# Expert weights in larger adjacent pieces: 4 KB of gate and up, 8 KB of down, a strided read of the columns, and sorted row counts in both layers

## The reference

```python
def grouped_moe(h, router_w, router_bias, w_gate, w_up, w_down, sh_gate, sh_up, sh_down):
    ...                                   # sigmoid scores, best group of four experts, top 2 in it
    out = swiglu(t, sh_gate, sh_up, sh_down)            # the shared expert, every token
    for e in range(N_EXPERTS):                          # 16
        out = out + combine[:, e:e + 1] * swiglu(t, w_gate[e], w_up[e], w_down[e])
def swiglu(t, wg, wu, wd):
    return (jax.nn.silu(t @ wg) * (t @ wu)) @ wd        # wg, wu: 1024 x 512, wd: 512 x 1024
```

## Time and profile before

| | |
|---|---|
| median of three runs | 1674.37 us |
| the profiled execution's own time | 1667.71 us |
| its span, first to last instruction | 1665.8 us |
| TensorE busy | 1504.8 us, 90% |
| VectorE, ScalarE, GpSimd busy | 528.6, 393.8, 187.7 us |
| mean granted TensorE clock | 0.961 of full speed |
| moved by DMA | 334.6 MB, mean 201 GB/s |
| sparse steps of layer 0 | from 784.7 us, about 284 us |
| sparse steps of layer 1 | from 1340.8 to 1631.8 us |

### The profile page before, as it was taken

One profiled execution on the slowest core, in us unless ns is written; L12 is line 12 of the kernel. 1 busy time (PEld: TensorE's weight loads), 2 busy tenths in 40 slices (PEclk: granted clock), 3 DMA queues, 4 the chain that ended last, 5 costly groups with the idle time before them and its releaser, 6 DMA issues.

```text
span 1665.8 us, 31618 instructions
## 1 busy us (share of the span) xinstructions
PE 1504.8 (90%) x13895; PEld 868.5 (52%) x13895; DVE 528.6 (32%) x934; ACT 393.8 (24%) x930; POOL 187.7 (11%) x207
## 2 busy tenths in 40 slices
PE   4799888999988999799999999978989899999996
PEld 2434444454545444455555555545647865555555
DVE  3254555445433121224112112141352412111213
ACT  2211333333434200210122122112241212122111
POOL 0000034133332200000000100000000010100100
PEclk9599999999989999889999999998999899999998
DMA  7355334333330622015999999961302189999972
GB/s 275 127 185 191 126 104 149 104 125 127 127 127 26 170 82 76 3 51 214 388 373 362 377 370 380 361 215 56 109 1 77 66 321 391 372 361 358 366 258 85
DMA packets 161871, 334.62 MB, mean 201 GB/s; under 512 B 14083, under 2 KB 61883, under 8 KB 155579
## 3 DMA queue, kind: packets, MB, share of 16 engines
q1 hardware_dynamic: 148795, 308.77, 52.3%
q0 software_dynamic: 7104, 12.60, 2.2%
q10 hardware_dynamic: 5824, 11.11, 1.9%
HBM read 327.58 MB, written 16.65 MB: 207 GB/s over the span
## 4 chain that ended last, share of the span: by engine, by line
PE 84%; ACT 6%; DVE 5%; DMA 3%; issue 1%; SPq 0%; DVEq 0%; ACTq 0%; POOLq 0%
PE ps L1365 19%; PE ps L1076 10%; PE ps L1395 10%; PE ps L1093 7%; PE ps L1288 7%; PE ps L1319 5%; PE ps L1027 3%; PE ps L1181 2%; PE ps L1600 2%; PE ps L1409 2%; PE ps L1512 2%; PE ps L1046 2%; PE ps L1129 1%; ACT aT L736 1%; PE ps L1168 1%
## 5 line engine op out<-in xcount | busy, mean ns | idle before, releaser
L1365 PE MATMUL ps<-ring,ssb 128*32 128x256 f32 x3472 | 193.3, 379 | 1.6 <-ACT ssb L891 1.6
L1076 PE MATMUL ps<-aT,ring 128*128 128x512 f32 x384 | 175.4, 606 | 0.0
L1365 PEld LDWEIGHTS ps<-ring,ssb 128*32 128x32 f32 x3472 | 113.9, 110 | 75.0 <-ACT ssb L891 1.8
L2010 DVE COPY big<-ps 32x256 f32<-32x256 f32 x190 | 80.5, 424 | 201.6 <-PE ps L1395 199.5
L1076 PEld LDWEIGHTS ps<-aT,ring 128*128 128x128 f32 x384 | 71.6, 194 | 84.3 <-issue 84.2
L1395 PE MATMUL ps<-ring,ssb 128*32 128x256 f32 x1808 | 105.4, 389 | 11.0 <-ACT ssb L903 11.0
L1093 PE MATMUL ps<-aT,ring 128*128 128x512 f32 x256 | 114.2, 595 | 0.0
L908 ACT COPY big<-ps 32x256 f32<-32x256 f32 x190 | 68.8, 362 | 179.7 <-PE ps L1395 177.9
L1288 PE MATMUL ps<-big,ring 128*128 128x512 f32 x256 | 110.2, 592 | 0.0
L2003 DVE TENSOR_TENSOR ssb<-ssb,ps 128x384 f32<-128x384 f32 (+2 forms) x32 | 17.6, 551 | 267.1 <-ACT ssb L899 267.1
L808 ACT ACTIVATE ssb<-ps,ncum 128x128 f32<-128x128 f32 x256 | 73.3, 371 | 98.5 <-PE ps L1156 97.6
(11 more groups left out here) (293 smaller groups left out, 1875.8 us busy)
## 6 DMA issues: line engine op xcount, KB each, us to landing
ring<-in_ada_w SPq DMA_DIRECT2D x48, 1024.0 KB
ring<-in_moe_w_gate SPq DMA_DIRECT2D x75, 512.0 KB, 9.2
ring<-in_moe_w_up SPq DMA_DIRECT2D x75, 512.0 KB, 12.1
ring<-in_moe_w_down SPq DMA_DIRECT2D x37, 1024.0 KB, 10.3
ring<-in_ssd_in_w SPq DMA_DIRECT2D x20, 1024.0 KB
tmp<-in_moe_w_down SPq DMA_DIRECT2D x14, 1024.0 KB
ssb<-in_moe_w_gate SPq DMA_DIRECT2D x27, 512.0 KB, 8.2
ssb<-in_moe_w_up SPq DMA_DIRECT2D x27, 512.0 KB, 10.5
```

Of the source, the lines that this page charges most:

```text
L1076: ins = pe.matmul(ps[:, bank, :], slot(u)[:, k, (i % 2) * P:(i % 2 + 1) * P], aT[:, k, :], start=(k == 0), stop=(k == KD - 1))
L1365: ins = pe.matmul(tiled_gu[32 * c:32 * c + 32, g, :].rearrange("p (r n) -> p r n", r=2), XgT[l][:, k * C + 32 * g:k * C + 32 * g + 32], pa ...
L2010: ins = dve.tensor_copy(Y[s % 2][32 * g:32 * g + 32, 256 * c:256 * c + 256], tiled_y[32 * c:32 * c + 32, g, :])
```

## The change

- In the sparse path (`together`), partition p gets adjacent rows of the weights. Unit j of gate and up holds rows 8p+2j and 8p+2j+1, which is one piece of 4 KB for each of the two; unit j of down holds rows 4p+2(j-4) and the next, one piece of 8 KB. The dense path and the shared expert keep their row blocks.
- So that contraction index and rows agree, `mtok` is written in another order of features (ScalarE's copy at L929 reads PSUM with a stride of 8 elements), and hidden unit 4p+c must be at partition p of block c: the moving operand of L1365 for column tile c is now every fourth column, starting with c. `pair_slot` has gate or up outside and k inside.
- Both layers sort their experts by counts, in steps with rows of a table, and SyncE reads the expert's name in both. Layer 0 has three steps of 128 rows, seven of 96 and six of 64; layer 1 one of 128, four of 96, eight of 64 and three of 32. In layer 1 expert 0 is still loaded ahead and gets the first rank by a large constant in its key. The flag compares each step's count with its rows.
- Tables come per layer with `val` in HBM. On the dense path the experts loaded ahead are loaded again (`loaded_again`), since their layout differs.

```diff
-CAP = [128, 96]
-BIG, SMALL = 3, 4
-RANK_OF = [0, 15, 1, 14, 2, 13] + list(range(BIG, 13))
+RANK_ROWS = [[128] * 3 + [96] * 7 + [64] * 6, [128] + [96] * 4 + [64] * 8 + [32] * 3]
+RANK_OF = [[0, 15, 1, 14, 2, 13, 3, 12, 4, 11, 5, 6, 10, 7, 8, 9], [0, 13, 1, 5, 2, 6, 3, 7, 4, 8, 9, 10, 11, 12, 14, 15]]
+AHEAD_EXPERTS = [0, 1]
 def step_rows(l, s):
-    if l:
-        return CAP[l]
-    return CAP[0] if RANK_OF[s] < BIG else 64 if RANK_OF[s] >= NE - SMALL else 96
+    return RANK_ROWS[l][RANK_OF[l][s]]
...
         def pair_slot(u):
-            return room[u.slot].rearrange("p (k r n) -> p k r n", k=2, r=2)
+            return room[u.slot].rearrange("p (r k n) -> p k r n", k=2, r=2)
...
-            def weights(u, j, gate, up, down):
+            def weights(u, j, gate, up, down, together=False):
                 if j < 4:
                     for r, src in enumerate((gate, up)):
-                        sp_.dma_start(pair_slot(u)[:, :, r, :], src[2 * j * P:2 * (j + 1) * P, :].rearrange("(k p) n -> p k n", p=P))\
-                            .then_inc(s_w[u.slot], 16)
+                        src = src.rearrange("(p k) n -> p k n", p=P)[:, 2 * j:2 * j + 2, :] if together else \
+                            src[2 * j * P:2 * (j + 1) * P, :].rearrange("(k p) n -> p k n", p=P)
+                        sp_.dma_start(pair_slot(u)[:, :, r, :], src).then_inc(s_w[u.slot], 16)
+                elif together:
+                    sp_.dma_start(slot(u, 2), down.rearrange("(p k) n -> p k n", p=P)[:, 2 * (j - 4):2 * (j - 3), :])\
+                        .then_inc(s_w[u.slot], 16)
...
                 for r in range(2 * nt):
                     act.wait_ge(s_mt8, 8 * l + r + 1)
-                    act.copy(mtok[:, r // 2, (r % 2) * 512:(r % 2 + 1) * 512], ps[:, (4, 7)[r % 2], :]).then_inc(s_mtv, 1)
+                    act.copy(mtok[:, r // 2, :].rearrange("p (k c q) -> p k c q", k=KD, c=KD)[:, :, 4 * (r % 2):4 * (r % 2) + 4, :],
+                             ps[:, (4, 7)[r % 2], :].rearrange("p (c q k) -> p k c q", c=4, k=KD)).then_inc(s_mtv, 1)
...
                                 ins = pe.matmul(tiled_gu[32 * c:32 * c + 32, g, :].rearrange("p (r n) -> p r n", r=2),
                                                 XgT[l][:, k * C + 32 * g:k * C + 32 * g + 32],
-                                                pair_slot(u)[:, k % 2, :, c * P:(c + 1) * P],
+                                                pair_slot(u)[:, k % 2, :, :].rearrange("p r (n c) -> p r c n", c=4)[:, :, c, :],
                                                 start=(k == 0 and g % 2 == 0), stop=(k == KD - 1), skip_group_check=True)
...
             def place(l):
-                if l:
-                    link(dve.tensor_reduce(sl[l][0][0:1, 0:1], count[0:1, :], AX.X, ALU.max))
-                    dve.tensor_scalar(flag[0:1, 0:1], sl[l][0][0:1, 0:1], float(C), None, ALU.is_gt).then_inc(s_flag, 1)
-                    return
...                                       # the sorting chain, now for both layers, with the last part new:
-                link(dve.tensor_scalar(over, pos1, BIG + 0.5, -32.0, ALU.is_lt, ALU.mult))
-                link(dve.scalar_tensor_tensor(out=over, in0=count, scalar=-96.0, in1=over, op0=ALU.add, op1=ALU.add))
-                link(dve.tensor_scalar(key, pos1, NE - SMALL + 0.5, 32.0, ALU.is_gt, ALU.mult))
-                link(dve.tensor_tensor(key, key, over, ALU.add))
+                link(dve.tensor_tensor(pprod[l], permT[l], count.unsqueeze(1).to_broadcast([P, NE, NE]), ALU.mult))
+                link(dve.tensor_reduce(count_s[l], pprod[l], AX.X, ALU.add))
+                link(dve.tensor_tensor(count_s[l], count_s[l], rows[l], ALU.subtract))
...
             def indices(l):
-                if l:
-                    dve.tensor_copy(gidx[0:C, 0:NE], sl[l][2][0:C, :]).then_inc(s_gi, 1)
-                    dve.scalar_tensor_tensor(out=sidx[0:C, 0:NE].unsqueeze(2), in0=slots[l][0:C, :, 2:3], scalar=float(T), in1=row,
-                                             op0=ALU.mult, op1=ALU.add).then_inc(s_gi, 1)
-                    return
```

More of the change, by code:

```diff
@@ L164, in host_constants @@
     c16 = np.concatenate([ident, mask_f, mask_b] + am + [sel], axis=1).astype(np.float32)
-    erev = np.concatenate([np.arange(NE, 0, -1), np.arange(4, 0, -1), 1 + k, 1 + np.array(RANK_OF)])
-    erev = np.tile(erev.astype(np.float32), (P, 1))
+    erev = np.tile(np.concatenate([np.arange(NE, 0, -1), np.arange(4, 0, -1), 1 + k]).astype(np.float32), (P, 1))
     val = np.zeros((P, NT, NE, 3), np.float32)
@@ L170, in host_constants @@
     val[..., 1] = 1 + np.arange(NT)[None, :, None]
-    return c32, c16, erev, val.reshape(P, -1)
+    ranks = np.zeros((2, P, 3, NE), np.float32)
+    for l in range(2):
+        ranks[l, :, 0] = np.arange(NE, 0, -1)
+        ranks[l, :, 0, 0:AHEAD_EXPERTS[l]] += 1 << 20
+        ranks[l, :, 1] = 1 + np.array(RANK_OF[l])
+        ranks[l, :, 2] = [step_rows(l, s) for s in range(NE)]
+    val = np.concatenate([np.tile(val.reshape(1, P, -1), (2, 1, 1)), ranks.reshape(2, P, -1)], axis=2)
+    return c32, c16, erev, val
 class Unit:
@@ L323, in build @@
         val = [tmp[:, c:c + 96].bitcast(BF16).rearrange("p (t e v) -> p t e v", t=NT, e=NE) for c in (5120, 3072)]
[L324 to L330, removed]
+        valf = [tmp[:, c:c + 240] for c in (5248, 3168)]
+        tie, rank1, rows = ([valf[l][:, c:c + 16] for l in range(2)] for c in (192, 208, 224))
+        rank = [tmp[:, c:c + 64] for c in (5488, 3408)]
+        slots = [tmp[:, c:c + 48].rearrange("p (e v) -> p e v", e=NE) for c in (5552, 3472)]
+        sl = [[tmp[:, c + 16 * n:c + 16 * n + 16] for n in range(4)] for c in (5600, 3520)]
+        key, pos1, count_s, names = ([v[:, 16 * n:16 * n + 16] for v in (tmp[:, 5664:5728], rt[15])] for n in range(4))
+        permT, pprod = ([tmp[:, c:c + 256].rearrange("p (s e) -> p s e", e=NE) for c in cs2] for cs2 in ((5728, 3584), (6144, 3840)))
         QT = big[:, 0:2048].rearrange("p (c n) -> p c n", c=8)
@@ L460, in pair_slot, with arrived, loaded_again @@
         def pair_slot(u):
-            return room[u.slot].rearrange("p (k r n) -> p k r n", k=2, r=2)
-        def arrived(eng, u, n=0):
-            eng.wait_ge(s_w[u.slot], u.arrived + n * u.step)
+            return room[u.slot].rearrange("p (r k n) -> p k r n", k=2, r=2)
+        def arrived(eng, u):
+            eng.wait_ge(s_w[u.slot], u.arrived)
+        def loaded_again(l, u):
+            return sum(x.step for s in range(AHEAD_EXPERTS[l]) for j in range(6) for x in units["x", l, s, j] if x.slot == u.slot)
         block = ctx.enter_context(nc.Block())
@@ L520, in shared, with expert @@
                     held[u.slot] = unit_free(name, j)
-            def expert(l, s, js, free, w):
-                for j in js:
+            def expert(l, s, free, w, together):
+                for j in range(6):
                     u = units["x", l, s, j][0]
@@ L529, in expert @@
                         sp_.wait_ge(s_gi, 3)
-                    weights(u, j, *w)
+                    weights(u, j, *w, together)
                     held[u.slot] = free(l, s, j)
@@ L551, in after, with moe @@
                     held[u.slot] = unit_free(name, v)
-            def moe(l, ahead, following):
+            def moe(l, following):
                 shared(l, f"sgu{l}", 0)
-                for s in range(ahead):
-                    expert(l, s, range(6), tiled_free, static(l, s))
+                for s in range(AHEAD_EXPERTS[l]):
+                    expert(l, s, tiled_free, static(l, s), True)
                 sparse = choose(sp_, l)
@@ L560, in moe @@
                 with sp_.If(sparse):
-                    for s in range(ahead, NE):
-                        expert(l, s, range(6), tiled_free, static(l, s) if l else permuted(s))
+                    for s in range(AHEAD_EXPERTS[l], NE):
+                        expert(l, s, tiled_free, permuted(l, s), True)
                     after(l, following, True)
@@ L566, in moe @@
                     held.update(at_branch)
-                    for s in range(ahead):
+                    for s in range(AHEAD_EXPERTS[l]):
                         for j in range(6):
-                            held[units["x", l, s, j][0].slot] = dense_free(l, s, j)
-                    for s in range(ahead, NE):
-                        expert(l, s, range(6), dense_free, static(l, s))
+                            u = units["x", l, s, j][0]
+                            held[u.slot] = s_w[u.slot], u.arrived
+                    for s in range(NE):
+                        expert(l, s, dense_free, static(l, s), False)
                     after(l, following, False)
@@ L1307, in unit, with dense_arrived @@
                     return units["x", l, e - 1, j][0] if e else units[f"sgu{l}"][j]
+                def dense_arrived(e, j):
+                    u = unit(e, j)
+                    pe.wait_ge(s_w[u.slot], u.arrived + (loaded_again(l, u) if e else 0))
```

(4 more changed lines are left out.)

53 lines of the change are left out of this document (26 added, 27 removed).

## The result

The changed kernel takes 1892.53 us (median of 4 runs, 1890.4 to 1894.15) against 1674.68 for the kernel before (4 runs, 1674.22 to 1676.28): ratio 1.1298 [1.1279, 1.1318], 218 us slower. The profiled execution took 1891.26 us, its span is 1889.5 us. The forecast was 1622; what came is rival 1, which was priced at 1870, and the measured time lies 17 us above the end of the range (1876).

The account below looks back on a forecast made before the run. Bound taken: TensorE, with 7% DMA slack behind it. Terms -10 - 47.6 - 1.7 + 2.5 + 1 + 3 = -52.8 us took the profiled 1667.71 to 1615, forecast 1622 beside the median (chance 0.38); range 1603 to 1876, likeliest case 1605 to 1654.

Parts of the forecast that it names:

- rival 1: Gate and up (L1365): the strided read doubles its time, +196 us in all, 1870 us; chance 0.36.
- The strided moving operand: Gate and up reads float32 at a step of 16 bytes: taken as costing nothing, ends nothing and twice.
- Layer 0: Layer 0's sparse steps: fewer rows give -10 us, ends -2 and -11.
- Layer 1: Layer 1's sparse steps: fewer rows, then bound by DMA at 410 GB/s, ending at 1584.1: -47.6 us.
- The shared down product: After layer 1's steps: units land 5 us later, the 7 us product has room beside scatter and read back.
- The tail: Last step: one group copied out instead of three, two VectorE copies instead of six, -1.7 us.
- Small additions: ScalarE's strided PSUM copies to token rows +2.5 us, layer 1's later first gather +1, TensorE's clock +3.
- the late gather: Start of layer 1: sorting and indices put the first gather 3 us later, mostly hidden, +1 us taken.
- The clock's 3 us: Layer 1: TensorE waits for weights and may lose clock; none to 12 us, 3 taken.
- R: DMA rate in layer 1 with larger pieces: 410 GB/s chosen, between 391 and 425.
- rival 3: DMA: larger pieces bring nothing, rate stays 391 GB/s, layer 0's ring runs dry at times; -33, 1641 us; chance 0.12.
- estimate of 400: DMA rate in layer 1 by the skill's packet cost: pieces only some 2.5% faster, 400 GB/s, total 6 us worse.

Follow-up runs that it names:

- e1: The changed kernel with the moving operand of gate and up read contiguously again (wrong values, same work): 1639.56 us, 0.9797 of the kernel before.
- e9: The kernel before with the strided read alone (wrong values, same work): 2035.13 us, beside 1683.26 for the kernel before.
- e5: e2 with the gate and up operand read at a step of 12 bytes in layer 1 alone (wrong values, same work): 1666.7 us.
- e6: e2 with the gate and up operand read at a step of 32 bytes in layer 1 alone (wrong values, same work): 1733.79 us.
- e2: e1 with down in row blocks and 4 KB pieces everywhere, contiguous read, computes the reference: 1642.73 us, 0.9814 of the kernel before.
- e4: The changed kernel with the sorted row counts alone; pieces, token rows and contiguous read as before: 1651.32 us, 0.9867 of the kernel before.
- e8: e2 with layer 1's shared expert reading moving (chunks 0, 1) or stationary operand (chunks 2, 3) at a step of 4 float32: 1653.86 us.

## Why the prediction was wrong, by its own steps

**The strided moving operand** is the step that failed: "Between the two I take nothing". Of its two ends, nothing and twice, the value taken was the wrong one; the true factor is 2.10, 5% above the upper end. The reason given was that the arithmetic spends two clock periods on each column and so leaves the reader time. It spends 0.846 ns, and the reader needs 1.78. The row nearest in access, VectorE's 1.75 ns per element, had the number within 2%, and I set it aside because its engine was another. That it came so near is in part luck: it is 14 ns over eight elements, and 1 ns more or less in the two means it comes from would move it by 0.12. Runs e1, e9, e5 and e6 show it. With 7.28 instead of 2 x 3.46 us a group, rival 1 would have had 29 us more, 1899: that it came out 7 lower lies mostly in the execution (1891.26 profiled, 1892.53 median, 1.3 apart where I had added 6.7), the rest in the small terms.

**What the strided read swallowed.** From e1 to the changed kernel 80 groups x 3.82 = 305.6 us were added, and the span grew by 252.5. Layer 0's steps took 283.7 in e1, so they grew by 162.9 (45 groups are 171.9); layer 1's 258.6, so +91.2 (35 are 133.7). The 9 us missing in layer 0 and the 42 in layer 1 are for the most part e1's waits for weights, 6.0 and 25.5 us, which went when TensorE became the bound again, as rival 1 said. In layer 1 there were also records at TensorE's low clock: in e1 its gate and up cost 60.2 ns each, against 55.4 in layer 0.

**The rest of the sum, read from e1** (-52.8 forecast; its spans give -28.8, its medians -34.3):

- *Layer 0*: -10 forecast, -1.8 measured (285.5 to 283.7), just beyond the pessimistic end. TensorE waited 6.0 us for weights, and its records took 7.0 us less, not 11.1. The waits for the slots stand in the chain of e1 twice:

```profile
943.84 21.25 DMA ssb<-in_moe_w_up
...
996.33 23.01 DMA ring<-in_moe_w_up
```

- *Layer 1*: steps -32.3 (290.9 to 258.6) where -47.6 was forecast; they ended at 1599.46, not 1584.1. Nearly all of that is the DMA. From the first load at 1337.65 to the landing of the last down unit at 1597.22 it took 259.6 us, where 239.8 + 3 + 1.5 = 244.3 was counted: it moved 100.5 MB at 387 GB/s, not 98.3 MB at 410. What moved beyond the 98.3 MB includes part of the shared down units, which were issued from 1580.55 on and ran beside the last down unit. The rate was 405 in the middle, but 381 to 392 up to 1450, with 20 us at 309 in the first step of 128 rows, which held slots. Against the 390 after them those 20 us cost about 4, near the 3 I gave them; why the rest of the start was slower than the middle stays open, and it was so in e2 and e4 too (386 and 374 GB/s in 1400 to 1425). After the landing came 2.2 us where I had 0.9, since TensorE had dropped to its 1.2 GHz level (granted 0.50) and the half of the down product took 1.93:

```profile
1360.00:1380.00 20.00, 19.50 (x353) 11.75 (x349) 5.08 (x12) 4.55 (x13) 2.09 (x3) 1.00 0.88 309
...
1590.00:1600.00 10.00, 7.46 (x65) 2.40 (x57) 0.75 (x3) 1.00 (x4) 0.10 (x1) 0.50 0.68 280
```

- *The shared down product* was said to take 7 us and to have room. It takes 14.08 before, from 1631.63, twice the 7, and there ends just ahead of the pairs' arrival at 1647.3: it had no room. The units did land 5 us behind the last down unit, as forecast (1602.19). Put behind that wait, and on a TensorE whose clock was 0.63 in 1600 to 1610, it is the end of the chain in e1:

```profile
1581.64 20.55 DMA ring<-in_shared_w_down
1602.19 0.14 issue
1602.33 16.54 PE ps L1426 x64
1618.87 2.02 PE ps L1434 x18
```

The tail thus grew by 3.4 us (34.1 to 37.5) instead of shrinking by 1.7; in the changed kernel, where TensorE stays busy and doesn't wait for these units, it shrank by 1.8.

- *Small additions*: ScalarE's copies 0, not 2.5. Between the layers +2.4 in e1, where 1 was given to the late gather. TensorE did wait 1.5 us for it, `1335.66 3.24 DMA ssb<-m_rows,gidx` in the chain, and before it, from 1322.69 on, the chain is VectorE's sorting of layer 1, where in the kernel before it was TensorE's own work; the rest is within what this stretch varies by. The clock's 3 us can't be separated: in 1500 to 1550 TensorE waited for weights and kept 1.00, from 1570 on it had 0.66, 0.67 and 0.50.
- *R*: 405 GB/s in the middle of layer 1 against 410 chosen, between the rates of rival 3 (391) and of 8 KB alone (425). Over the whole of layer 1 it was 387. The estimate of 400 from the Trainium skill's cost per packet (DMA: Bandwidth & Descriptors, "Why small descriptors are slow (HBM only)") was as near in the middle and nearer on the whole; redone for the mix of pieces it gives 1.9% and 399, still an estimate. As a gain it is too small: the same stretch shows 5.5% (405 against 384). Rival 3 is refuted as a mechanism, since size moved the rate from 384 to 405 and the time from e4 to e1 by 11.8 us, but its time, 1641, is about what e1 has (1639.56), by luck: layer 0, the rate at the start and the tail took what the pieces gave.

**The chances.** Rival 1 had 0.36 and its mechanism, place and scale were right. The range ended at 1876 because the factor was taken as exactly 2; a bound read from another engine deserved some width of its own. The forecast's own 0.38 still stood above it.

## What to carry to other kernels

Don't lay out float32 weights so that TensorE's moving operand takes one value out of each 16 bytes. Up to a step of two the read is nearly free (5%), from three on it is paid at 1.8 ns per new 16 bytes, and one strided tile among four costs as much as four. Where an order must be changed, change it in rows, as e2 does with the contraction; on the stationary side the same step cost 0.7 us for 32 records (e8). And weigh a layout by what it is for: 8 KB pieces in place of 4 were worth 3 us at most, the read that they forced 250. When an experiment of one line can split a change, the rest of it may be a gain that was buried.

## What was not expected of the hardware

- TensorE's moving reader and VectorE come out nearly alike for a new 16 bytes, 1.78 and 1.75 ns, VectorE's from a difference of 14 ns only.
- The duration of a strided record (633 ns) grows by 254 ns over 379, not by the factor 2.1 of the pace; the ratio of the mean durations (1.67) understates the loss, the busy time per record shows it.
- ScalarE reads PSUM at a step of 32 bytes with no loss (588 ns for 512 elements in both).
- Pieces of 2 KB (gate and up) and 4 KB (down) gave 384 GB/s in the mixed traffic of layer 1, 4 and 4 KB 399, 4 and 8 KB 405; twice the size again for down brought 1.5% at most.
